# The opening of the feed-forward in a four-layer kernel: order of VectorE's work, and one convolution tap on ScalarE

## The reference

```
# layers 0 and 1
h = rms_norm(x, w);  x = x + (silu(h @ w_gate) * (h @ w_up)) @ w_down
# layers 2 and 3
h = rmsnorm(x, g);   gate, val = split(h @ w_up)
gate = b + sum(gate shifted by (-1, 0, 1)[j] * w[j] for j in range(3))
x = x + (silu(gate) * val) @ w_down
```

## Time and profile before

| | us |
|---|---|
| median of 3 runs (2412.42 to 2412.76) | 2412.7 |
| the profiled execution, its own time | 2414.04 |
| its span | 2412.3 |
| mean granted TensorE clock | 0.992 of full |

### The profile page before, as it was taken

One profiled execution on the slowest core, in us unless ns is written; L12 is line 12 of the kernel. 1 busy time (PEld: TensorE's weight loads), 2 busy tenths in 40 slices (PEclk: granted clock), 3 DMA queues, 4 the chain that ended last, 5 costly groups with the idle time before them and its releaser, 6 DMA issues.

```text
span 2412.3 us, 35999 instructions
## 1 busy us (share of the span) xinstructions
PE 2358.0 (98%) x14456; PEld 2036.8 (84%) x14456; DVE 1679.7 (70%) x2336; ACT 1081.1 (45%) x1685; POOL 514.1 (21%) x343
## 2 busy tenths in 40 slices
PE   9999999999999999999999999999999999999999
PEld 8877889999877789999887777889888777788988
DVE  6876686776587678677676758746567675774654
ACT  5565343434466434334445743433344574442432
POOL 3013130221200303113332320311312202031230
PEclk9999999999999999999999999999999999999999
DMA  5211133233211122323222011332332201133232
GB/s 190 71 36 36 62 114 105 93 116 100 97 53 36 53 70 101 110 91 113 95 88 71 19 53 63 109 108 88 105 105 88 70 20 53 57 114 109 88 105 88
DMA packets 33718, 201.46 MB, mean 84 GB/s; under 512 B 3856, under 2 KB 4112, under 8 KB 16144
## 3 DMA queue, kind: packets, MB, share of 16 engines
q1 hardware_dynamic: 33120, 198.63, 24.2%
q10 hardware_dynamic: 432, 0.53, 0.1%
HBM read 197.05 MB, written 2.10 MB: 83 GB/s over the span
## 4 chain that ended last, share of the span: by engine, by line
PE 84%; DVE 10%; DVEq 2%; issue 2%; ACT 1%; POOL 0%; ACTq 0%; DMA 0%
PE bank L2190 17%; PE bank L2192 17%; PE bank L2191 17%; PE bank L2483 7%; PE bank L2484 7%; PE bank L2485 7%; PE bank L2336 2%; PE bank L2373 2%; PE bank L2397 2%; DVE a_conv L1585 1%; PE bank L2319 1%; DVE neg_max L1945 1%; DVE w_lo L1044 1%; PE bank L2384 1%; DVE b_p L1976 1%
## 5 line engine op out<-in xcount | busy, mean ns | idle before, releaser
L1044 DVE TENSOR_TENSOR w_lo<-w_all,w_hi 128x2048 fp32r<-128x2048 f32 (+3 forms) x142 | 291.1, 2050 | 123.6 <-ACT w_hi L406 122.5
L406 ACT ACTIVATE w_hi<-w_all 128x2048 fp32r<-128x2048 f32 (+3 forms) x142 | 234.0, 1648 | 272.8 <-PE bank L2192 235.2
L2190 PE MATMUL bank<-act_hi,w_hi 128*128 128x512 f32 x704 | 276.7, 393 | 6.3 <-DVE act_lo L1232 6.3
L2191 PE MATMUL bank<-act_lo,w_hi 128*128 128x512 f32 x704 | 276.3, 392 | 0.0
L2192 PE MATMUL bank<-act_hi,w_lo 128*128 128x512 f32 x704 | 275.8, 392 | 0.0
L2060 POOL TENSOR_TENSOR w_all<-w_all 128x512 f32<-128x512 f32 x54 | 79.5, 1471 | 912.4 <-DMA w_all<-weights 912.4
L2190 PE MATMUL bank<-h_ffn_hi,w_hi 128*128 128x512 f32 x544 | 212.6, 391 | 0.0
L2191 PE MATMUL bank<-h_ffn_lo,w_hi 128*128 128x512 f32 x544 | 211.8, 389 | 0.0
L2192 PE MATMUL bank<-h_ffn_hi,w_lo 128*128 128x512 f32 x544 | 211.7, 389 | 0.0
L1067 DVE TENSOR_TENSOR residual<-bank,residual 128x512 f32<-128x512 f32 x160 | 110.1, 688 | 143.3 <-PE bank L2192 140.6
L2190 PE MATMUL bank<-w_hi,h_mix_hi 128*128 128x512 f32 (+2 forms) x484 | 177.8, 367 | 2.5 <-DVE w_lo L1044 2.0
(11 more groups left out here) (422 smaller groups left out, 6293.5 us busy)
## 6 DMA issues: line engine op xcount, KB each, us to landing
w_all<-weights SPq DMA_DIRECT2D x136, 1024.0 KB, 4.9
w_all<-weights SPq DMA_DIRECT2D x48, 768.0 KB, 4.3
w_all<-weights SPq DMA_DIRECT2D x16, 512.0 KB, 3.6
w_all<-weights SPq DMA_DIRECT2D x4, 544.0 KB, 3.7
w_all<-weights SPq DMA_DIRECT2D x8, 256.0 KB, 6.7
x_out<-residual SPq DMA_DIRECT2D x8, 256.0 KB, 2.0
residual<-x_in SPq DMA_DIRECT2D x6, 256.0 KB, 7.2
cst<-consts SPq DMA_DIRECT2D x1, 966.0 KB, 8.8
```

The lines of the kernel that those rows point to most:

```text
L406: nc.scalar.activation(w_hi[s][:, cols], w_raw[s][:, cols], ACT.Copy).then_inc(w_hi_done, 1)
L1044: nc.vector.tensor_tensor(w_lo[s][:, cols], w_raw[s][:, cols], w_hi[s][:, cols].bitcast(F32), ALU.subtract).then_inc(w_ready, 1)
L2190: mm(out, ahi, bhi, start=start, stop=False)
L2191: mm(out, ahi, blo, start=False, stop=False)
```

## The change

Layers 0 and 1: in the loop over `dq` VectorE prepares group g + 2 ahead of the additions for `dq` 0 and 1, behind them for `dq` 2 and 3. The first seven-product group (`OPENING`) gets all four weight sums from VectorE (`all_weight_sums`), ahead of the additions of `dq` 2; GpSimd leaves it out.

Layers 2 and 3: in the plain pairs ScalarE computes the middle tap with its bias from `gate` (as it does for the later tiles from PSUM), and VectorE adds the two outer taps when both gate tiles have been scaled. VectorE prepares ahead of the additions for every `dq`. Input sums 1 and 3 move from the second plain pair behind the additions of `dq` 1; their high parts move on ScalarE from the second pair ahead of the preparation of `dq` 2; the four `t_lo` move behind the additions of `dq` 2 and behind the loop. The whole inputs are waited for alone ahead of the plain gate group, the sums only ahead of the first seven-product group. Counts of semaphores follow.

```diff
@@ -60,6 +60,7 @@
 ORDER = {g: n for n, g in enumerate(SEVEN)}
+OPENING = [FIRST[_lay] + IN_A + 2 * QUARTERS + CHUNKS[0] for _lay in range(LAYERS)]
 TOTAL = FIRST[-1]
@@ -291,6 +292,7 @@
+        gate_raw, opening_sums = sem("gate_raw"), sem("opening_sums")
@@ -335,9 +337,17 @@
-        def conv_tile(lay, f):
-
-            return (FT - CHUNKS[0]) * (lay - LAYERS) + f - lay * FT - CHUNKS[0]
+        def conv_tile(f):
+
+            return f - LAYERS * FT
+
+        def pool_order(g):
+
+            return ORDER[g] - sum(1 for o in OPENING if o < g)
+
+        def later_tile(f):
+
+            return f - LAYERS * FT - CHUNKS[0] * (f // FT - LAYERS + 1)
@@ -530,6 +540,13 @@
+                if b:
+                    for j in range(2):
+                        act.wait_ge(gate_raw, f - LAYERS * FT - (lay - LAYERS) * (FT - CHUNKS[0]) + j + 1)
+                        c = f - lay * FT + j
+                        nc.scalar.activation(silu[j][:, :], gate[j][:, 1:SEQ + 1], ACT.Identity,
+                                             bias=par_b[:, lay - LAYERS, B_CB + c:B_CB + c + 1],
+                                             scale=par_b[:, lay - LAYERS, B_CW + FT + c:B_CW + FT + c + 1]).then_inc(tap_done, 1)
                 for j in range(2):
@@ -546,7 +563,10 @@
                 s = g % 2
-                act.wait_ge(w_sums_a, ORDER[g] + 1)
+                if g in OPENING:
+                    act.wait_ge(opening_sums, OPENING.index(g) + 1)
+                else:
+                    act.wait_ge(w_sums_a, pool_order(g) + 1)
                 act.wait_ge(bank_done, 2 * (g - 2) + (1 if g - 2 in ORDER else 2))
@@ -644,9 +664,9 @@
-                def all_sums():
-
-                    for n in range(4):
+                def first_sums():
+
+                    for n in range(2):
                         input_sums_hi(lay, n)
@@ -659,11 +679,11 @@
-                    act.wait_ge(taps_done, conv_tile(lay, f) + j + 1)
+                    act.wait_ge(taps_done, later_tile(f) + j + 1)
                     act.activation(silu[j][:, :], silu[j][:, :], ACT.Silu).then_inc(conv_silu_done, 1)
                 plain_pair(lay, True, g, f, 0)
-                plain_pair(lay, True, g + 2, f + 2, 1, all_sums)
+                plain_pair(lay, True, g + 2, f + 2, 1, first_sums)
                 g += 4
@@ -671,6 +691,9 @@
                             whole_inputs_hi(k)
+                    if dq == 2:
+                        for n in (2, 3):
+                            input_sums_hi(lay, n)
                     prepare(g + 2, True)
@@ -1205,18 +1228,18 @@
                     if b:
-                        dve.drain()
+                        dve.drain().then_inc(gate_raw, 1)
+                    else:
+                        dve.drain().then_inc(gate_ready, 1)
+                if b:
+                    for j in range(2):
                         c = c0 + j
                         cw = [par_b[:, lay - LAYERS, B_CW + tap * FT + c:B_CW + tap * FT + c + 1] for tap in range(3)]
-                        cb = par_b[:, lay - LAYERS, B_CB + c:B_CB + c + 1]
                         s_ = silu[j][:, :]
-                        nc.vector.tensor_scalar(s_, gate[j][:, 1:SEQ + 1], cw[1], cb, ALU.mult, ALU.add)
-                        dve.drain()
+                        dve.wait_ge(tap_done, conv_tile(f) + j + 1)
                         nc.vector.scalar_tensor_tensor(s_, gate[j][:, 0:SEQ], cw[0], s_, ALU.mult, ALU.add)
                         nc.vector.scalar_tensor_tensor(s_, gate[j][:, 2:SEQ + 2], cw[2], s_, ALU.mult, ALU.add).then_inc(gate_ready, 1)
-                    else:
-                        dve.drain().then_inc(gate_ready, 1)
                 split_lo(g + 2)
@@ -1237,8 +1260,8 @@
                 _, s2, a11, a12, _, a21, s4 = (w_all[s][:, n * BLOCK:(n + 1) * BLOCK] for n in range(7))
-                if g < FIRST[LAYERS]:
-                    dve.wait_ge(w_sums_a, ORDER[g] + 1)
+                if g < FIRST[LAYERS] and g not in OPENING:
+                    dve.wait_ge(w_sums_a, pool_order(g) + 1)
                     nc.vector.tensor_tensor(a21, a11, a21, ALU.subtract)
@@ -1260,6 +1283,18 @@
+            def all_weight_sums(g):
+
+                s = g % 2
+                s1, s2, a11, a12, a22, a21, s4 = (w_all[s][:, n * BLOCK:(n + 1) * BLOCK] for n in range(7))
+                dve.wait_ge(w_in[s], 16 * (g // 2))
+                nc.vector.tensor_tensor(s1, a21, a22, ALU.add)
+                dve.drain()
+                nc.vector.tensor_tensor(s2, s1, a11, ALU.subtract).then_inc(opening_sums, 1)
+                nc.vector.tensor_tensor(a21, a11, a21, ALU.subtract)
+                dve.drain()
+                nc.vector.tensor_tensor(s4, a12, s2, ALU.subtract).then_inc(w_sums_b, 1)
+
             def normalised_inputs(lay, ks):
@@ -1278,7 +1313,7 @@
-                dve.wait_ge(seven_hi, inputs_at(lay) + n + 1)
+                dve.wait_ge(seven_hi, inputs_at(lay) + n + 1 + (KT if lay >= LAYERS and n >= 2 else 0))
                 m = (0, 2, 1, 3)[n]
@@ -1373,17 +1408,22 @@
                 for dq in range(QUARTERS):
+                    if dq < 2:
+                        prepare(g + 2, True)
                     if dq == 0:
                         input_sums_lo(lay, 2)
+                    if dq == 2:
+                        all_weight_sums(g + 2)
                     for half in range(2):
                         add_tile(lay, g, half, 2 * dq + half)
-                    prepare(g + 2, dq < QUARTERS - 1)
                     if dq == 0:
                         inputs_lo(lay, 2)
+                    if dq >= 2:
+                        prepare(g + 2, dq == 2)
                     g += 1
@@ -1427,7 +1467,7 @@
-                    dve.wait_ge(seven_hi, inputs_at(lay) + 4 + k + 1)
+                    dve.wait_ge(seven_hi, inputs_at(lay) + 2 + k + 1)
                     nc.vector.tensor_tensor(h_ffn_lo[:, k, :], h_norm[:, k, :], h_ffn_hi[:, k, :].bitcast(F32), ALU.subtract).then_inc(seven_ready, 1)
@@ -1435,41 +1475,38 @@
                     before, after = (par_b[:, lay - LAYERS, B_CW + tap * FT + c:B_CW + tap * FT + c + 1] for tap in (0, 2))
-                    dve.wait_ge(tap_done, conv_tile(lay, f) + j + 1)
+                    dve.wait_ge(tap_done, conv_tile(f) + j + 1)
                     nc.vector.scalar_tensor_tensor(s_[:, 1:SEQ], src[:, 0:SEQ - 1], before, s_[:, 1:SEQ], ALU.mult, ALU.add)
-                def last_sums():
-
-                    input_sum(1)
-                    dve.drain()
-                    input_sum(3)
-                    input_sums_lo(lay, 0)
-
                 plain_pair(lay, True, g, f, 0, 0, lambda: normalised_inputs(lay, range(KT // 2)))
                 dve.drain()
-                plain_pair(lay, True, g + 2, f + 2, 1, 2, last_sums)
-                input_sums_lo(lay, 1)
+                plain_pair(lay, True, g + 2, f + 2, 1, 2)
                 g += 4
                 for dq in range(QUARTERS):
-                    if dq == 0:
-                        input_sums_lo(lay, 2)
+                    prepare(g + 2, True)
+                    if dq < 2:
+                        for k in range(4 * dq, 4 * dq + 4):
+                            whole_inputs_lo(k)
                     for half in range(2):
                         add_tile(lay, g, half, 2 * dq + half)
-                    prepare(g + 2, True)
-                    if dq == 0:
-                        input_sums_lo(lay, 3)
-                    if dq in (0, 1):
-                        for k in range(4 * dq, 4 * dq + 4):
-                            whole_inputs_lo(k)
+                    if dq == 1:
+                        input_sum(1)
+                        dve.drain()
+                        input_sum(3)
+                    if dq == 2:
+                        for n in (0, 1):
+                            input_sums_lo(lay, n)
                     g += 1
+                for n in (2, 3):
+                    input_sums_lo(lay, n)
                 for chunk, n in list(enumerate(CHUNKS))[1:]:
@@ -2125,7 +2162,7 @@
                 for g in SEVEN:
-                    if FIRST[lay] <= g < FIRST[lay + 1]:
+                    if FIRST[lay] <= g < FIRST[lay + 1] and g not in OPENING:
                         weight_sums(g)
@@ -2568,11 +2605,13 @@
                     if chunk == 1:
-                        pe.wait_ge(seven_ready, inputs_at(lay + 1))
+                        pe.wait_ge(seven_ready, inputs_at(lay) + KT)
                     for i in range(size // 2 if chunk >= 1 else 0):
                             feature_half(g, j, h_ffn_hi, h_ffn_lo, KT)
+                        if chunk == 1 and i == 0:
+                            pe.wait_ge(seven_ready, inputs_at(lay + 1))
                         u = g + 1
```

(4 more changed lines are left out.)

## The result

| us | before | after |
|---|---|---|
| median, 6 runs each | 2412.7 | 2422.2 |
| the profiled execution, its own time | 2414.0 | 2427.9 |
| its span | 2412.3 | 2426.1 |

The ratio is 1.0042 (95% interval 1.0029 to 1.0056): slower by 9.5 us. The forecast said +9.7, slower. The profiled execution of after is the slowest of its six runs, so its terms are set against medians where that matters.

The account below looks back on a forecast made before the run. TensorE, busy 98% of the span, bounds the kernel, so only its idle and slow-clock time can be won. Layers 2 and 3 +5.8 and layers 0 and 1 +3.9 make +9.7: 2412.7 to 2422.4 us, range 2411 to 2426.

Parts of the forecast that it names:

- layers 2 and 3: Feed-forward openings there: one stall removed, a later one added, +2.9 us per layer, +5.8 in all.
- layers 0 and 1: Ahead of the first seven-product group: VectorE's longer chain delays it, +2.1 and +1.8 us, +3.9 in all.
- The wait for `act_lo`: TensorE's wait in the first down projection of layers 2 and 3: goes, -6.3 us per layer, clock part included.
- D0 to D3: The four groups of the first down projection; in layers 2 and 3 forecast to run at full clock.
- P: Plain group behind the first down projection, layers 2 and 3: starts after 6.2 us idle, plus 2.9 us of slow clock.
- Contention: VectorE operations with two SBUF inputs and GpSimd's weight sums take turns, costing 1.1 us each.
- turn-taking misses: Rival, all openings: VectorE and GpSimd collide less; 2413.2 us with fewest collisions, 2418 with half; chance 0.18.
- more stalls: Rival: the first seven-product group of layers 2 and 3 becomes late too, over 2426 us; chance 0.06.
- the clock: TensorE's clock halves after each opening stall; in layers 2 and 3 this costs 2.9 us per stall.
- S: First seven-product group, layers 0 and 1: forecast wait ahead of it 5.6 us instead of 3.5 and 3.8.
- as before: Layers 0 and 1: the clock falls either way, so the slow-clock cost behind the opening stall stays unchanged.
- The stall at P doesn't come: Rival, layers 2 and 3: twice -6.3 us, layers 0 and 1 as forecast, 2404 us; chance 0.12.

Follow-up runs that it names:

- e1: The changed kernel with layers 0 and 1 put back as before, so only the part in layers 2 and 3: 2420.4 us (1.0028).
- e2: The kernel before with only the part of the change in layers 0 and 1: 2415.3 us (1.0013).
- e3: The changed kernel with ScalarE making `w_hi` of P ahead of the high parts of input sums 1 and 3: 2415.2 us (1.0011).
- e4: The changed kernel with GpSimd's first sums of each layer's feed-forward held until `w_lo` of P or S is made: 2420.4 us (1.0032).
- e5: The changed kernel, layers 0 and 1 as before, input sums 1 and 3 in VectorE's gap, their high parts earlier on ScalarE, `t_lo` spread: 2408.2 us (0.998).
- e10: The kernel before with only the middle tap of the plain pairs moved to ScalarE: 2412.6 us (0.9998).
- e6: The changed kernel, layers 2 and 3 as before, third and fourth weight sums behind `w_lo` of S, last down-projection additions ahead of its `e_lo`: 2411.9 us (0.9994).
- e7: e5 with GpSimd's first sums held until `w_hi` of P is made: 2414.5 us (1.0006).

## Why the prediction came out

| term | forecast | measured |
|---|---|---|
| layers 2 and 3 | +5.8 | +7.4 (e1) |
| layers 0 and 1 | +3.9 | +2.4 (e2) |
| together | +9.7 | +9.5 |

The intervals of the halves, +4.3 to +9.2 and +1.0 to +5.3, hold the forecast terms. That these were off in opposite directions rests on the profiles below.

- **The mechanism in layers 2 and 3 was right, link by link.** The wait for `act_lo` goes; D0 to D3 run at full clock; P waits for an addition behind `w_lo` of P behind `w_hi` of P behind `t_hi`. e3 shows ScalarE's part of it (2.6 us of D0 to P), e4 GpSimd's (1.6), e5 that with the sums and their `t_hi` in the gap there is no stall.
- **Contention was right in kind and near in size:** sums +0.92 and `w_lo` +0.73 in layer 2, where I had 1.1 each; third and fourth weight sum 1.79 and 1.60 (1.8 each). The rival "turn-taking misses" didn't come. Nor did "more stalls": after, TensorE waits no more than 0.1 us between P and the next down projection. The idleness is 5.25 instead of 6.2 since the chain is 0.4 us shorter by these two, and since D3 ends 0.6 later than I put it (0.4 at the start of D2, which I had at 0.1: VectorE's first addition of D0 ends at 1509.1 and D2 starts at 1509.25; the rest is the last matmul's own length).
- **The term mis-sized is the clock.** I took one number, 2.9 us per stall, from one execution, for the stall removed and for the stall added. The removed one costs 1.7 in a second execution, with the rest paid in attention; the new one costs 1.6 in layer 2 and 2.65 in layer 3 after, and about 2.7 in e1. The clock was low for 6.8 us where it cost about 2.7 to 2.9, and for 3.4 us where it cost 1.6 to 1.7. Per layer, e1 against the second execution of before: the stall removed is worth 1.2 us less than forecast, D0 to P ends 0.4 sooner, the slow clock behind P costs 0.2 less, attention 0.3 more; +0.9, where the medians want 0.8.
- **Layers 0 and 1:** D0 to S grew by 1.8 in each (2.1 and 1.8 forecast), and what is behind S got shorter by 0.5 and 1.0 us in the profile of after, as the slow clock behind S lasted 4.8 instead of 5.8 us in layer 0 and 3.7 instead of 5.9 in layer 1. That the clock part would be "as before" failed. In e2's own profile the part behind S is 0.6 and 0.4 shorter than before, which makes 2.5 of the whole, and the medians say 2.4. Against the second execution of before it would be 0.7 longer in layer 1, so this part is no firmer than the clock. That 1.5 too much here cancels 1.6 too little above is luck.
- **"The stall at P doesn't come"** was priced at 2404. e5 built it, with layers 0 and 1 as before, for which that price is 2400: measured 2408.2. Removing two stalls of 6.3 us gives 4.7, not 12.6. In e5's profile D0 to P is 5.3 and 5.4 us shorter than in the first execution of before, and P to the next down projection 1.5 longer, so by the openings alone a layer gains 3.8 to 3.9. Some of the price was a clock part that is paid elsewhere, and some comes back ahead of and inside the first seven-product group (0.5 and 0.6 us in e5), where VectorE's work now crowds. How much each of them takes isn't separated.

## What to carry to other kernels

A wait named in the profile is removed by doing its releaser's work earlier, but the work it was queued behind has to go somewhere: follow it to the next hand-off between engines, in each engine's own order, before calling the wait won. Here two input sums fitted a gap that VectorE had anyway (2408.2), and 13 us later they stood ahead of a hand-off (2420.4, the same half of the change). A clock part is not a constant of a stall: size it from more than one execution, and judge by whole layers.

## What the runs showed of the hardware

- **The same stall, different clock costs.** The granted clock fell after 2.4, 3.2 and 5.0 us of idleness, and came back 3.2 to 6.0 us after work had begun again. Behind stalls of 2.6 us (both in e3, and layer 2 of e10) and one of 2.0 us (layer 1 of e6) it fell 0.9 to 1.4 us after work had begun again. Ahead of S in layer 0 of e1, e5 and e10 it stayed full through 3.3 to 3.6 us of idleness. The length of a stall alone doesn't tell what it costs.
- **The clock's cost moves.** In two executions of one kernel, 1.2 us less behind D0 came with 1.5 to 1.7 more in attention ahead of it, and whole layers agreed to 0.3 us.
- **Turns.** Where both had work waiting, VectorE lost 0.7 to 1.1 us per turn to a sum of GpSimd, and GpSimd 0.8 to VectorE (2.10 in place of 1.27 for its second sum in layer 2 after). Holding GpSimd back moved the turns: no gain clear of the noise in e4, 6.2 us lost in e7 against e5.
